# A two-layer SSM and delta-net block after a transformer block, in split fp32: norm factors as rows, spread over partitions by transfers

## What is computed

```python
for l in range(DEPTH_2):                                  # 2 layers
    h = h + 0.5 * swiglu(rms_norm_2(h, ffn1_norm[l]), ffn1_w_in[l], ffn1_w_out[l])
    u = rms_norm_2(h, mix_norm[l])
    (z_s, xbc, dt_s, qkv, z_d, b_d, a_d, gate_s, gate_d) = jnp.split(u @ w_in[l], split_points, axis=-1)
    y_s = mamba2_branch(z_s, xbc, dt_s, ...)              # its last step: rms norm over 4 groups of 512
    y_d = deltanet_branch(qkv, z_d, b_d, a_d, ...)        # q, k: l2 norm over 128, 8 heads each
    merged = (jax.nn.sigmoid(gate_s) * (y_s @ ssm_w_branch[l])
              + jax.nn.sigmoid(gate_d) * (y_d @ dn_w_branch[l]))
    h = h + merged @ w_out[l]
    h = h + 0.5 * swiglu(rms_norm_2(h, ffn2_norm[l]), ffn2_w_in[l], ffn2_w_out[l])

def l2_norm(x):
    return x * lax.rsqrt(jnp.sum(x * x, axis=-1, keepdims=True) + EPS)
```

## Time and profile before

| | |
|---|---|
| median of 3 runs | 2365.84 us (2362.18 to 2369.88) |
| the profiled execution | 2371.16 us, its span on the core 2369.3 us |
| TensorE busy | 2263.5 us (96%) |
| DVE, ACT busy | 1395.8 us (59%), 1124.8 us (47%) |
| mean granted TensorE clock | 0.981 of full speed |
| HBM read | 361.68 MB, 153 GB/s over the span |

### The profile page before, as it was taken

One profiled execution on the slowest core, in us unless ns is written; L12 is line 12 of the kernel. 1 busy time (PEld: TensorE's weight loads), 2 busy tenths in 40 slices (PEclk: granted clock), 3 DMA queues, 4 the chain that ended last, 5 costly groups with the idle time before them and its releaser, 6 DMA issues. The chain is left out here.

```text
span 2369.3 us, 39840 instructions
## 1 busy us (share of the span) xinstructions
PE 2263.5 (96%) x15164; PEld 2026.1 (86%) x15164; DVE 1395.8 (59%) x1879; ACT 1124.8 (47%) x1615; POOL 43.0 (2%) x40
## 2 busy tenths in 40 slices
PE   6999889999999998999999999999998989999998
PEld 5887778878879988999998887888988989998887
DVE  3436465565558976475556555556978357456555
ACT  3453544454455565432545445445556551435444
POOL 0000000000000000000000000000000000000000
PEclk8999999999999999999999999999999999999999
DMA  9652245545553423211355554553532321144553
GB/s 396 237 214 95 93 153 182 194 161 194 190 182 143 177 72 107 92 70 54 129 192 185 192 181 177 183 189 143 180 122 92 124 91 52 58 176 178 195 179 131
DMA packets 50696, 364.65 MB, mean 154 GB/s; under 512 B 5760, under 2 KB 5760, under 8 KB 6656
## 3 DMA queue, kind: packets, MB, share of 16 engines
q1 hardware_dynamic: 47664, 341.97, 39.8%
q0 software_dynamic: 2896, 20.78, 2.3%
HBM read 361.68 MB, written 1.05 MB: 153 GB/s over the span
## 5 line engine op out<-in xcount | busy, mean ns | idle before, releaser
L1316 ACT ACTIVATE HI<-ring 128x1024 fp32r<-128x1024 f32 x630 | 649.0, 1054 | 916.5 <-PE bank L448 468.0
L1834 DVE TENSOR_TENSOR LO<-ring,HI 128x1024 fp32r<-128x1024 f32 x342 | 418.1, 1225 | 369.0 <-ACT HI L1316 368.7
L1840 DVE TENSOR_TENSOR LO<-ring,HI 128x2048 fp32r<-128x2048 f32 x139 | 318.4, 2291 | 312.8 <-ACT HI L1316 312.8
L446 PE MATMUL bank<-UH,HI 128*128 128x256 f32 x1584 | 462.6, 292 | 1.2 <-DVE LO L1834 1.2
L447 PE MATMUL bank<-UL,HI 128*128 128x256 f32 x1584 | 451.3, 285 | 0.0
L448 PE MATMUL bank<-UH,LO 128*128 128x256 f32 x1584 | 451.1, 285 | 0.0
L480 PE MATMUL bank<-HI,UH 128*128 128x512 f32 x896 | 350.2, 391 | 7.1 <-DVE LO L1840 4.9
L482 PE MATMUL bank<-HI,UL 128*128 128x512 f32 x896 | 349.3, 390 | 0.0
L481 PE MATMUL bank<-LO,UH 128*128 128x512 f32 x896 | 349.3, 390 | 0.0
L446 PEld LDWEIGHTS bank<-UH,HI 128*128 128x128 f32 x1584 | 307.3, 194 | 10.6 <-issue 9.0
L447 PEld LDWEIGHTS bank<-UL,HI 128*128 128x128 f32 x1584 | 307.5, 194 | 1.2 <-issue 1.2
(11 more groups left out here) (302 smaller groups left out, 3272.4 us busy)
## 6 DMA issues: line engine op xcount, KB each, us to landing
ring<-in_w_stream SPq DMA_DIRECT2D x315, 1024.0 KB, 4.8
ARENA<-in_ada_stream POOLq DMA_DIRECT2D x16, 1024.0 KB, 5.1
ARENA<-in_ada_stream SPq DMA_DIRECT2D x8, 1024.0 KB, 14.8
ARENA<-in_na_bias POOLq DMA_DIRECT2D x2, 1024.0 KB, 14.8
ARENA<-in_ropes POOLq DMA_DIRECT2D x1, 1088.0 KB, 20.4
H<-in_x_tok SPq DMA_DIRECT2D x1, 1024.0 KB, 5.2
out_tok<-SQ SPq DMA_DIRECT2D x4, 256.0 KB, 2.1
PK<-in_pack POOLq DMA_DIRECT2D x2, 384.5 KB, 4.5
```

Of the source, the lines that this page charges most:

```text
L446: nc.tensor.matmul(out, lh, rh, start=start, stop=False, **kw)
L1316: nc.scalar.activation(HI[:, q % PARTS, at], ring[:, q % RING, at], ACT.Copy).then_inc(hi_ready, 1)
L1834: nc.vector.tensor_tensor(LO[:, q % PARTS, at], ring[:, q % RING, at], HI[:, q % PARTS, at].bitcast(F32), ALU.subtract).then_inc(lo_ready, 1)
L1840: nc.vector.tensor_tensor(LO[:, q % PARTS, :], ring[:, q % RING, :], HI[:, q % PARTS, :].bitcast(F32), ALU.subtract).then_inc(lo_ready, 2)
```

## The change

Four sets of factors go another way.

1. Sums. A sum of squares is now a matmul with 32 weight columns, all zero but one that is all ones (`ONEHOT`, a slice of 32 out of 64 columns), and 256 moving columns. It gives the sum as a row on one partition of a 32-partition group, for all 256 tokens. Heads or groups go to the four 32-partition groups in turn. `head_sums2` does four heads in four matmuls; `group_sums(p)` does two groups in eight; the eight output heads take eight. The old matmuls with 128 weight columns are gone.
2. Roots and reciprocals are now of 128 x 256 tiles (`QROOT`, `GROOT`, `OROOT`), one per eight heads or four groups.
3. Spreading. `qk_spread` and the spreading of the output factors are gone from TensorE. POOL stores the tile of rows (128 x 256) to HBM, waits for that, and loads it back broadcast over 128 partitions in parts of 512 KB: two each for q, k and the outputs, one for the groups. POOL's layer loop is unrolled.
4. Order. TensorE waits for `yrms_ready` and `qk_ready` only after the first z_d panel (`late_panel(0)`), and the halves of the later ones move. DVE norms q and k at j = 6 and 7, four pairs each; it does the group reciprocal after `late_low(0)`; it does the split of one more panel before it norms the outputs. The four reciprocals in `group_norm` are gone.
5. At the start, the eight first modulation panels share four semaphores in pairs.

```diff
-                for j in range(L_ZS): ...
-                                mm = squares_summed(QSQ[:, pr, e, :], 2 * pr + e, qss)
-                    if j % 2 == 1 and j >= 3:
-                        group_sum((j - 3) // 2)
-                    if 4 <= j:
-                        qk_spread(2 * j - 8)
-                        qk_spread(2 * j - 7)
-                group_sum(3)
-                pe.wait_ge(yrms_ready, 4 * l + 4)
-                pe.wait_ge(qk_ready, 8 * l + 8)
+                def one_hot(row):
+                    return ONEHOT[:, 31 - row:63 - row]
+                def head_sums2(c):
+                    pe.wait_ge(qksq_ready, 8 * l + 2 * c + 2)
+                    for g in range(4):
+                        mm = nc.tensor.matmul(bank[6 + c // 2][32 * g:32 * g + 32, 0:S], one_hot(c), QSQ[:, 2 * c + g // 2, g % 2, :],
+                                              start=(c % 2 == 0), stop=(c % 2 == 1))
+                def group_sums(p):
+                    pe.wait_ge(ysq_ready, 4 * l + 2 * p + 2)
+                    for e in range(4):
+                        for g in (2 * p, 2 * p + 1):
+                            mm = nc.tensor.matmul(bank[0][32 * g:32 * g + 32, 0:S], one_hot(0), SQ[:, at:at + S], ...)
+                    if 1 <= j <= 4:
+                        mm = head_sums2(j - 1)
+                    if j == 5:
+                        group_sums(0)
+                group_sums(1)
...
+                late_panel(0)
+                pe.wait_ge(yrms_ready, l + 1)
+                pe.wait_ge(qk_ready, 8 * l + 8)
                 head_products(0)
                 head_products(1)
-                late_panel(0)
+                late_panel(1)
...
+                def spread_factors(n, ready, value, src, loads):
+                    pool.wait_ge(ready, value)
+                    pool.dma_start(norm_rows_at[n], src).then_inc(factors_stored, 16)
+                    pool.wait_ge(factors_stored, 16 * (4 * l + n + 1))
+                    rows = norm_rows_at[n].rearrange("(g r) n -> r g n", r=32)
+                    for c, to, loaded in loads:
+                        pool.dma_start(to, rows[c].unsqueeze(0).to_broadcast([P, 4, S])).then_inc(loaded, 16)
...
                 def group_norm(g):
-                    dve.wait_ge(yrms_ready, 4 * l + g + 1)
-                    need(step(nc.vector.reciprocal(GRMS[:, g, :], GRMS[:, g, :])))
+                    dve.wait_ge(group_factors, 16 * l + 16)
...
                 dve.wait_ge(orms_ready, l + 1)
-                nc.vector.reciprocal(QR[:, :, 0:8], QROOT[:, :, 0:8]).then_inc(or_ready, 1)
+                nc.vector.reciprocal(OROOT, OROOT).then_inc(or_ready, 1)
                 late_low(L_ZD + L_GATES - END_GATES + 1)
+                late_low(L_ZD + L_GATES - END_GATES + 2)
+                dve.wait_ge(out_factors, 32 * l + 32)
                 for j in range(4):
```

More of the change, by code:

```diff
@@ L247, in build_program @@
         uh_ready, ul_ready = sem("uh_ready"), sem("ul_ready")
-        ada1_loaded = [sem(f"ada1_loaded{i}") for i in range(ADA_FIRST)]
+        ada1_loaded = [sem(f"ada1_loaded{i}") for i in range(ADA_FIRST // 2)]
         ada2_loaded = [sem(f"ada2_loaded{i}") for i in range(2)]
@@ L304, in build_program @@
             sem("qksq_ready"), sem("qkss_done"), sem("qkrms_ready"), sem("qk_ready"))
-        qkr_ready, qkb_done, or_ready, ob_done = sem("qkr_ready"), sem("qkb_done"), sem("or_ready"), sem("ob_done")
+        qkr_ready, or_ready, gr_ready = sem("qkr_ready"), sem("or_ready"), sem("gr_ready")
+        factors_stored, q_factors, k_factors = sem("factors_stored"), sem("q_factors"), sem("k_factors")
+        group_factors, out_factors = sem("group_factors"), sem("out_factors")
         kk_done, gseg_ready, gdec_ready, grow_ready, weights_ready, aqk_ready, qd_ready = (
@@ L413, in _ @@
             split(Q_FFN0 + 1)
-            with pool.Fori(0, LAYERS) as l:
+            for l in range(LAYERS):
                 pool.wait_ge(ul_ready, KT * (FILL_LAYER + 4 * l))
@@ L427, in _ @@
                                             spread(END_A[:, 8 * g:8 * g + 8], HD), ALU.mult).then_inc(xend_ready, 1)
+                def spread_factors(n, ready, value, src, loads):
[5 more added lines that the diff above has]
+                        pool.dma_start(to, rows[c].unsqueeze(0).to_broadcast([P, 4, S])).then_inc(loaded, 16)
+                for b in range(2):
+                    spread_factors(b, qkr_ready, 2 * l + b + 1, QROOT[:, b, :],
+                                   [(2 * b + i, QFACTOR[:, 8 * b + 4 * i:8 * b + 4 * i + 4, :], (q_factors, k_factors)[b])
+                                    for i in range(2)])
+                spread_factors(2, gr_ready, l + 1, GROOT, [(0, GRMS[:, :, :], group_factors)])
+                spread_factors(3, or_ready, l + 1, OROOT, [(i, OFACTOR[:, 4 * i:4 * i + 4, :], out_factors) for i in range(2)])
         @block.tensor
@@ L1221, in _ @@
                 keys_turn(1)
-                late_panel(3)
+                late_wide(3, 1)
                 for g in range(4):
@@ L1629, in _, with group_rms @@
                         conv_in(j, j % 2)
-                def group_rms(g):
-                    act.wait_ge(yss_done, 4 * l + g + 1)
-                    nc.scalar.activation(GRMS[:, g, :], bank[GROUP_BANKS[g]][:, 0:S], ACT.Sqrt,
-                                         bias=EPST[:, :]).then_inc(yrms_ready, 1)
+                def group_rms():
+                    act.wait_ge(yss_done, 2 * l + 2)
+                    nc.scalar.activation(GROOT, bank[0][:, 0:S], ACT.Sqrt, bias=EPST[:, :], scale=1.0 / 512).then_inc(yrms_ready, 1)
                 def group_squares(g):
@@ L1643, in qk_root @@
                     act.wait_ge(qkss_done, 2 * l + i + 1)
-                    nc.scalar.activation(QROOT[:, :, 8 * i:8 * i + 8], tiles(bank[6 + i][:, 0:16], 2),
-                                         ACT.Sqrt, bias=EPST[:, :]).then_inc(qkrms_ready, 1)
+                    nc.scalar.activation(QROOT[:, i, :], bank[6 + i][:, 0:S], ACT.Sqrt, bias=EPST[:, :]).then_inc(qkrms_ready, 1)
                 act.wait_ge(y_taken, 8 * l + 8)
@@ L1768, in _ @@
                         act.wait_ge(oss_done, l + 1)
-                        nc.scalar.activation(QROOT[:, :, 0:8], tiles(bank[6][:, 0:16], 2), ACT.Sqrt, bias=EPST[:, :],
-                                             scale=1.0 / P).then_inc(orms_ready, 1)
+                        nc.scalar.activation(OROOT, bank[6][:, 0:S], ACT.Sqrt, bias=EPST[:, :], scale=1.0 / P).then_inc(orms_ready, 1)
                 for j in range(1, END_GATES - 1):
@@ L1826, in _ @@
             nc.vector.memset(CPAD[:, :, :], 0.0)
+            need(step(nc.vector.memset(ONEHOT[:, :], 0.0)))
+            nc.vector.memset(ONEHOT[:, 31:32], 1.0)
             nc.vector.memset(EPST[:, :], EPS).then_inc(fills_done, 1)
@@ L2351, in _ @@
                         qk_reciprocal((j - 3) // 2)
-                    if j >= 4:
-                        qk_norm(2 * j - 8)
-                        qk_norm(2 * j - 7)
+                    if j >= 6:
+                        for pr in range(4 * j - 24, 4 * j - 20):
+                            qk_norm(pr)
                 def late_low(j):
@@ L2431, in right_side @@
                     ins.then_inc(rhs_ready, 1)
+                late_low(0)
+                dve.wait_ge(yrms_ready, l + 1)
+                nc.vector.reciprocal(GROOT, GROOT).then_inc(gr_ready, 1)
                 segments(0)
@@ L2438, in _ @@
                 first_inverse(1)
-                late_low(0)
+                late_low(1)
                 segments(2)
                 weights(2)
-                late_low(1)
+                late_low(2)
                 segments(3)
@@ L2449, in _ @@
                     decayed_queries(b)
-                late_low(2)
                 late_low(3)
```

85 lines of the change are left out of this document (29 added, 56 removed).

## The result

The changed kernel takes 2371.2 us (median, 2368.1 to 2373.2), the kernel before beside it 2369.3 us. The ratio is 1.0013, with a 95% interval of 1.0007 to 1.0019: no faster, if anything a hair slower, where 2331 was predicted. (That forecast started from the kernel before at 2365.8, the median of three executions; the twenty beside the changed kernel give 2369.3.) The profiled execution has a span of 2368.0 us, against 2369.3 before.

A forecast was written before the change was run, and what follows sets the result against it. TensorE, busy 96% of the span, was taken as the bound. Per layer -23.3 - 2.4 + 3.1 - 1.3 + 3.0 - 1.7 + 4.9 = -17.7 us, -35 for two, gave 2331 against 2365.8; range 2320 to 2352.

The forecast's parts named there:

- So factors and DVE are ready together, and the transfer is hidden: Layer's end: output factors arrive about 18 us behind panel END 0, with each load priced at 4.5 us.
- The estimate of 3.2 us per load: Output factors: the Trainium skill's 2.0 us plus bytes at 436 GB/s, bringing them at about 16 us, wait unchanged.
- the wait for LO: Second projection panel: TensorE newly waits for DVE's low half of the split, +3.7 us per layer.
- a last wait above 8 us: Sign that the prediction is wrong: the new wait at the second projection panel, expected at 3 to 5 us, exceeds 8.
- Store and two loads may take 8 more, and DVE asks for them 18 us behind it: z_d panels: q and k rows ready about 6.6 us behind the leading panel, so that panel hides their factors.
- if DVE waits for q or k factors: Sign that the prediction is wrong: DVE waiting for query or key factors in the z_d panels.
- The removed work: TensorE's sums and spreading: -24.4 us per layer, -23.3 after latency; new sums at 0.068 or 0.13 us per record.
- The idle time of 6.4: End of the z panels: TensorE idle 6.4 us before the last group sums, +3.1 us per layer net.
- half a fall: Before the third turned inverse and behind the second projection panel's wait: half of a 2.4 us clock loss, +1.2 each.
- Rival 1: Output factors late, at 22 to 25 us, for 2339 to 2345; with badly packed sums 2340 to 2357; chance 0.24.
- Rival 3: Almost no gain: saved TensorE time becomes idle as ACT or DVE paces the z panels; 2359 to 2370, chance 0.06.
- Rival 2: Slower than before through the output factors' wait alone, store and loads taking about 30 us; chance 0.05.

The follow-up runs named there:

- Run 2: Changed kernel with queries, keys and outputs multiplied by fixed numbers in place of their factors, transfers kept: 2347.0 us, 0.9904 to the kernel before.
- run 5: Changed kernel with the sixteen used rows stored so each load reads one unbroken 4 KB stretch: 2354.6 us, 0.9934 to the kernel before.

## Why the prediction was wrong

**The failed step** is "So factors and DVE are ready together, and the transfer is hidden", with its price for a load, 4.5 us from the nearest row. That row was a load from one stretch for each partition; the change's loads read four pieces 32 KB apart. One of them takes 7.3 to 7.8 us in an empty chip and two behind each other 9.7 to 10.5; in the kernel the outputs' two take 9.3 and 10.0, where the sum had 4.5. The store was priced well (2.1 against 2.08), and so the loads are nearly the whole miss. The estimate of 3.2 us per load that the prediction cites beside the sum would have missed by more (and with it the sum is 16.8, not 16): one piece took 3.5 to 3.8 us here. The factors came 22.8 us behind END 0, not 18; DVE stood 5.6 us for them; the wait for LO was 9.2 and 9.8 instead of 3.7. Run 2 takes just this away and finds 3.5. The prediction named a last wait above 8 us as a sign that it is wrong.

**The same price hid the second wait.** "Store and two loads may take 8 more, and DVE asks for them 18 us behind it" was said of queries and keys as one. The keys' reciprocal comes only at j = 5, 12 us behind the queries', and its store then lies on POOL's queue behind two slow loads (8.2 us). The keys' norm started 24.5 us after its reciprocal, and TensorE waited 3.0 and 5.5 us. By the rows the place behind the loads accounts for 6.3 us of the 24.5 (8.21 against 1.93 for the queries' store) and the keys' own two loads for 14.0; packed rows shorten both (run 5), so no run tests the place alone. The condition that would show this was in the prediction ("if DVE waits for q or k factors"), but the queue had not been walked for the second transfer.

**What held.** The removed work: 0.068 and 0.13 us per record were 0.067 to 0.08 and 0.12. The idle time of 6.4 (6.2 with fixed numbers), 3.6 ahead of the third turned inverse (3.7), 2.20 in the inverse chain nearly gone (0.42), no low clock behind the output sums (1.00 over the 15 us from 1124.66), and 3.7 at the second projection panel once the factors are there (3.5; the prediction's own terms, 24 + 2.0 + 2.3 less 24.1, give 4.2 rather than 3.7).

**What was mis-sized.** With fixed numbers the layers gain 13.1 and 12.1 us, not 17.7. The z panels give 10.6 instead of 12.5: sums that lie between panels cost 1.7 us in line before, not the 1.86 that a group's busy time divided by its blocks gives, and 0.64 after, not 0.55. The clock fell in full at both places where half a fall was booked. Behind the 3.71 us of idle time it was at 0.50 for at least 5.4 us (2.7 lost, 1.2 booked); behind the 3.5 at the projection 0.66 over 5 us (1.7 lost, 1.2 booked). The group sums behind the long idle time ran at the lower level and took 3.63 instead of 1.92: the prediction priced them at full clock and counted the lower level for the panel behind them only.

**The rivals.** Rival 1 named the mechanism (late output factors), but priced it at 22 to 25 us for 2339 to 2345; the 22.8 fits, and the time does not, since the keys' wait and the clock came on top. Rival 3 comes nearest in time (2359 to 2370 was its range, counted from a kernel before that is 3.5 us faster) with a reason that run 2 excludes. Rival 2's end, slower than before, was reached by 0.13% only, and without transfers of 30 us.

Where the gain went, of the 17.7 expected per layer: about 5 were never there, some 6 went at the second projection panel, 3 to 5.5 at the keys' norm, about 1 as a longer wait for the group squares (7.3 and 7.5 for 6.2). The 1.5 and 0.3 us that are left may be low clock behind these waits; no run separates that.

## What to carry to other kernels

When work leaves the engine that bounds a kernel for a transfer, walk the whole round with its queue: store, the loads behind it, and the next store behind those loads. Price a load by a row of the same access pattern, not of the same size. And when the profile says that idle time will appear where work was taken out, look for the next independent block that could stand there before booking it as a cost: here moving one panel was worth 8.8 us per layer behind the change, half of the 17.7 that the change was to give, and 4.5 and 5.9 without it. Two remedies were not tried: the keys' store on another engine's queue, and rows stored at other distances.

## What the hardware did that I had not expected

- A load of 512 KB, 4 KB to each partition, takes 3.5 us from one piece, 4.8 from four pieces 4 KB apart and 7.5 from four pieces 32 KB apart; that all 128 partitions read the same bytes costs some 0.4 us (3.7 against 3.3 from different places).
- Behind two such loads on POOL's queue a store of 128 KB lands after 8.2 us (10.3 in the second layer) instead of 1.9 (2.3).
- 16 one-column matmuls (32 records, 3.73 us) bring the granted clock down to 0.57 in the 4 us behind them though TensorE is never idle; 64 records of the 32-column form in 3.64 us leave it at 1.00.
- Behind a wait of 3.5 us at the same place, in kernels that differ only ahead of it, the clock was once at 0.66 over 5 us and once at 1.00.
- Matmuls of 32 rows in four row groups overlap 3.6 times at 256 columns (0.072 us per record against 0.258).
- The packed pair takes 8.0 us in the kernel and 5.5 to 6.0 in an empty chip; whether the panels' traffic is the reason was not tried.
